# First attention of a two-block transformer kernel: sinks as a score column, one score bank per head, another order in a step, query rounding on GpSimd

## What is computed

```python
def banded_attention(q, k, v, window, rel_table, sinks):
    ...
    def block(args):                     # one block of 128 queries, up to 256 keys
        ...
        s = jnp.einsum('bqhgd,bshd->bhgqs', qn, kn).astype(jnp.float32) + bias
        mask = in_win & (start - n_prev * BLOCK_Q + kj >= 0)
        s = jnp.where(mask, s, NEG_INF)
        ...
            sk = sinks.astype(jnp.float32).reshape(hkv, g_sz, 1, 1)
            m = jnp.maximum(jnp.max(s, axis=-1, keepdims=True), sk)
            e = jnp.exp(s - m)
            p = e / (jnp.sum(e, axis=-1, keepdims=True) + jnp.exp(sk - m))
        return jnp.einsum('bhgqs,bshd->bqhgd', p.astype(vn.dtype), vn)
```

## Time and profile before

| what | us |
|---|---|
| timed runs | 2120.36, 2120.88, 2125.22 |
| their median | 2120.88 |
| the profiled execution: its span, first to last instruction | 2123.0 |
| TensorE busy, whole span | 1988.0 (94%) |
| VectorE, ScalarE, GpSimd busy, whole span | 1021.4, 852.1, 797.5 |
| first attention, first score matmul to the projection's first matmul | 78.9 to 173.4 |
| DMA landing: one piece of raw queries; one bias tile | 2.9; 2.9 |

### The profile page before, as it was taken

How to read it: one execution, slowest core, us unless ns; L and a number is a source line. 1 busy time by engine, 2 the same in 40 slices (tenths; PEclk the granted TensorE clock), 3 DMA queues, 4 the chain that set the end, 5 groups by cost and what they waited for, 6 DMA issues and landing times.

```text
span 2123.0 us, 29194 instructions
## 1 busy us (share of the span) xinstructions
PE 1988.0 (94%) x9640; PEld 1642.4 (77%) x9640; DVE 1021.4 (48%) x2371; ACT 852.1 (40%) x1566; POOL 797.5 (38%) x368
## 2 busy tenths in 40 slices
PE   7889999999999899999999998999999889999896
PEld 5778788888778788878888886877887567777684
DVE  5483765421254767546553216657312664444414
ACT  4463422222343676542222224222223465555523
POOL 3323454444454100126444442545444223242340
PEclk9889999999999899999999999999999989999999
DMA  7432455422333112126553322322322112121121
GB/s 244 127 92 67 150 178 164 138 92 96 99 110 121 36 45 66 42 79 199 176 168 99 99 95 74 106 92 95 99 93 95 43 57 69 40 69 49 60 79 40
DMA packets 70011, 209.40 MB, mean 99 GB/s; under 512 B 9739, under 2 KB 15115, under 8 KB 69948
## 3 DMA queue, kind: packets, MB, share of 16 engines
q1 hardware_dynamic: 57724, 174.72, 25.7%
q10 hardware_dynamic: 12224, 33.85, 5.0%
HBM read 196.90 MB, written 8.49 MB: 97 GB/s over the span
## 4 chain that ended last, share of the span: by engine, by line
PE 58%; issue 21%; DVE 9%; POOL 9%; ACT 2%; DVEq 0%; POOLq 0%; ACTq 0%
PE bank L938 15%; PE bank L939 15%; PE bank L940 15%; POOL wsp L442 9%; PE bank L1215 3%; PE bank L1362 1%; PE bank L1199 1%; PE bank L1381 1%; PE bank L1188 1%; PE bank L1084 1%; PE bank L1373 1%; PE bank L1211 1%; PE bank L972 1%; PE bank L1061 1%; DVE gen L1614 0%
## 5 line engine op out<-in xcount | busy, mean ns | idle before, releaser
L442 POOL TENSOR_TENSOR wsp<-raw,wsp 128x1024 fp32r<-128x1024 f32 x294 | 730.6, 2490 | 1047.9 <-ACT wsp L515 1047.7
L938 PE MATMUL bank<-xs,wsp 128*128 128x512 f32 x1320 | 525.9, 398 | 36.0 <-DVE mid L2040 16.0
L939 PE MATMUL bank<-xs,wsp 128*128 128x512 f32 x1320 | 519.1, 393 | 0.0
L940 PE MATMUL bank<-xs,wsp 128*128 128x512 f32 x1320 | 518.9, 393 | 0.0
L515 ACT ACTIVATE wsp<-raw 128x1024 fp32r<-128x1024 f32 x294 | 307.3, 1052 | 234.4 <-PE bank L940 205.6
L938 PEld LDWEIGHTS bank<-xs,wsp 128*128 128x128 f32 x1320 | 251.3, 190 | 97.0 <-issue 32.3
L938 PE MATMUL bank<-xk,wsp 128*128 128x512 f32 x752 | 295.4, 393 | 9.5 <-DVE xk L1482 5.1
L939 PE MATMUL bank<-xk,wsp 128*128 128x512 f32 x752 | 294.5, 392 | 0.0
L940 PE MATMUL bank<-xk,wsp 128*128 128x512 f32 x752 | 294.4, 391 | 0.0
L940 PEld LDWEIGHTS bank<-xs,wsp 128*128 128x128 f32 x1320 | 250.8, 190 | 53.6
L939 PEld LDWEIGHTS bank<-xs,wsp 128*128 128x128 f32 x1320 | 251.4, 190 | 52.1 <-issue 1.4
(11 more groups left out here) (287 smaller groups left out, 2548.3 us busy)
## 6 DMA issues: line engine op xcount, KB each, us to landing
raw<-weights SPq DMA_DIRECT2D x294, 512.0 KB, 3.3
gen<-ada ACTq DMA_DIRECT2D x48, 512.0 KB, 3.7
tmp<-mid SPq DMA_DIRECT2D x64, 128.0 KB, 2.9
bias_b<-bias_row ACTq DMA_DIRECT2D x1, 4096.0 KB, 37.5
mid<-bias_b SPq DMA_DIRECT2D x8, 512.0 KB, 3.8
hT<-xT SPq DMA_DIRECT2D x2, 1024.0 KB, 10.3
bias_a<-bias_row ACTq DMA_DIRECT2D x1, 2048.0 KB, 16.9
mid<-bias_a SPq DMA_DIRECT2D x8, 256.0 KB, 2.9
```

Of the source, the lines that this page charges most:

```text
L442: pool.tensor_tensor(wsp[:, slot, 1, :], raw[:, slot, :], wsp[:, slot, 0, :].bitcast(F32), ALU.subtract).then_inc(w_ready, 1)
L938: pe.matmul(dst, w[0], x[0], start=first, stop=False)
L939: pe.matmul(dst, w[0], x[1], start=False, stop=False)
L940: return pe.matmul(dst, w[1], x[0], start=False, stop=last)
```

## The change

- The sink becomes column 256 of the score tile. The four score banks hold a zero in that column (four memsets before the stage, counted by `a_zero`), the bias tile holds the sink there (a copy of 128 x 2 per four steps), and the reduction and the Exp run over one column more. L1619, L1621, L1627 and L641 are gone, and `negsink` with them.
- Scores take four banks, one per head and parity (`bank[2 * b + e]`), and each head's scores, reduction and Exp are handed over on their own. Transposes have bank 4 alone, values banks 5 and 6, turned-out blocks bank 7 alone.
- In a slot TensorE does the scores first, then transposes, values and turning out.
- The rounding of queries goes from ScalarE to GpSimd (`pair_queries`), but for the very first pair. GpSimd does copy and subtraction for both heads of a pair in a row, after the scores that last read the old ones.
- SP loads the raw queries first, as soon as GpSimd is done with the old ones, and then the bias tile, each with its own semaphore.
- The two multiplies of `a_outputs` become one over both heads.

```diff
-TQ_A, TQ_B = 5 * 16, 6 * 16
+TQ_A, TQ_B = 4 * 16, 6 * 16
+SINK = 256
...
-        a_s = [gen[:, 1024 + 512 * b:1536 + 512 * b].rearrange("p (e k) -> p e k", e=2) for b in range(2)]
+        a_s = [gen[:, 3328 + 520 * b:3848 + 520 * b].rearrange("p (e k) -> p e k", e=2) for b in range(2)]
...
-                bias, chunk = bias_a[bass.ds((i + 4 * b) * 2, 2)].rearrange("h q y -> q h y"), qT[:, i * 2 + b, :]
+                bias = bias_a[bass.ds((i + 4 * b) * 2, 2)].rearrange("h q y -> q h y")
+                if not isinstance(i, int):
+                    sp.wait_ge(qs_ready, i * 4 + (2 * b - 2))
+                sp.wait_ge(q_ready, b + 1 if isinstance(i, int) else DC)
+                load_queries(b, qT[:, i * 2 + b, :])
                 if not isinstance(i, int):
                     sp.wait_ge(a_s_ready, i * 16 + (8 * b - 8))
-                sp.wait_ge(q_ready, b + 1 if isinstance(i, int) else DC)
-                sp.dma_start(tb[b][:, :, 0:256], bias).then_inc(tq_in[b], 16)
-                load_queries(b, chunk)
+                sp.dma_start(tb[b][:, :, 0:256], bias).then_inc(a_bias_in[b], 16)
...
+            def pair_queries(b, i):
+
+                for e in range(2):
+                    if i or b:
+                        pool.wait_ge(tq_in[b], i * TQ_A + TQ_A)
+                        if i:
+                            pool.wait_ge(a_qk, i * 16 + (8 * b - 8))
+                        pool.tensor_copy(qs[b][e][0], q_raw[b][e]).then_inc(qs_hi, 1)
+                    pool.wait_ge(qs_hi, i * 4 + (2 * b + e + 1))
+                    pool.tensor_tensor(qs[b][e][1], q_raw[b][e], qs[b][e][0].bitcast(F32), ALU.subtract
+                                       ).then_inc(qs_ready, 1)
+
             split_units(0, A_O + AHEAD)
-            queries_lo(0)
+            for n in range(PAIRS):
+                pair_queries(n % 2, n // 2)
...
             def a_soft(m, i):
 
-                b, w = m % 2, (128 if m % 4 == 0 else 256)
-                act.wait_ge(a_nm, i * 8 + (m + 1))
-                for e in range(2):
-                    x = act.activation(a_s[b][:, e, 0:w], a_s[b][:, e, 0:w], ACT.Exp, scale=-1.0,
-                                       bias=stat[:, b, 2 + e:3 + e], accum_out=stat[:, b, 4 + e:5 + e])
-                x.then_inc(a_p, 1)
-                act.wait_ge(a_sk, i * 8 + (m + 1))
-                act.activation(stat[:, b, 8:10], stat[:, b, 6:8], ACT.Exp).then_inc(a_sink, 1)
-
-                if m in (1, 2):
-                    queries_hi(1, m - 1, i * TQ_A + TQ_A)
-                if m in (5, 6) and not (isinstance(i, int) and i > 0):
-                    queries_hi(0, m - 5, i * TQ_A + 2 * TQ_A)
+                b, y0 = m % 2, (P if m % 4 == 0 else 0)
+                for e in range(2):
+                    act.wait_ge(a_s_ready, i * 16 + (2 * m + e + 1))
+                    act.activation(a_s[b][:, e, y0:SINK + 1], a_s[b][:, e, y0:SINK + 1], ACT.Exp, scale=-1.0,
+                                   bias=stat[:, b, e:e + 1], accum_out=stat[:, b, 4 + e:5 + e]).then_inc(a_p, 1)
...
-                act.activation(a_pt[b][:, :, 0:w], bank[2 + b].rearrange("p (e k) -> p e k", e=2)[:, :, 0:w],
+                act.activation(a_pt[b][:, :, 0:w], bank[4].rearrange("p (e k) -> p e k", e=2)[:, :, 0:w],
...
-                k0, w = max(blk - 1, 0) * P, (P if blk == 0 else 2 * P)
+                k0, y0 = max(blk - 1, 0) * P, (P if blk == 0 else 0)
                 for e in range(2):
                     for h in range(2):
-                        x = pe.matmul(bank[b][:, e * 256:e * 256 + w], qs[pp][e][h][:, blk * P:blk * P + P],
-                                      a_ks[:, pp, k0:k0 + w], start=h == 0, stop=h == 1)
-                x.then_inc(a_qk, 1)
+                        x = pe.matmul(bank[2 * b + e][:, y0:SINK], qs[pp][e][h][:, blk * P:blk * P + P],
+                                      a_ks[:, pp, k0:k0 + SINK - y0], start=h == 0, stop=h == 1)
+                    x.then_inc(a_qk, 1)
...
             def a_transpose(m, i):
-                b = m % 2
-                pe.wait_ge(a_p, i * 8 + (m + 1))
-                if again(i, m):
-                    pe.wait_ge(a_pt_ready, i * 8 + (m - 1))
-                for e in range(2):
+                b, y0 = m % 2, (P if m % 4 == 0 else 0)
+                if again(i, m, 1):
+                    pe.wait_ge(a_pt_ready, i * 8 + m)
+                for e in range(2):
+                    pe.wait_ge(a_p, i * 16 + (2 * m + e + 1))
                     for kb in range(1 if m % 4 == 0 else 2):
-                        x = pe.transpose(bank[2 + b][:, e * 256 + kb * P:e * 256 + kb * P + P],
-                                         a_s[b][:, e, kb * P:kb * P + P], ident[:, :])
+                        x = pe.transpose(bank[4][:, e * 256 + kb * P:e * 256 + kb * P + P],
+                                         a_s[b][:, e, y0 + kb * P:y0 + kb * P + P], ident[:, :])
...
-                        x = pe.matmul(bank[4 + b][:, e * HD:e * HD + HD], a_pt[b][:, e, kb * P:kb * P + P],
...
-                    pe.wait_ge(mid_ready, i * 2 + (m // 4 + 1))
-                pe.transpose(bank[6 + m // 4][:, blk * P:blk * P + P], a_o[b], ident[:, :]).then_inc(a_ot, 1)
+                    pe.wait_ge(mid_ready, i * 2 + (m // 4 + 2))
+                pe.transpose(bank[7][:, blk * P:blk * P + P], a_o[b], ident[:, :]).then_inc(a_ot, 1)
...
+            pe.wait_ge(a_zero, 4)
             in_steps(pe, 8, 6, lambda s, i, last: run_slot(
-                ((a_transpose, 2), (a_values, 3), (a_scores, 0), (a_turn_out, 4)), 8, s, i, last))
-            project_out(A_O, DC, XK_A, [0, 1, 2, 3, 4, 5], mid_ready, MID_A + DC)
+                ((a_scores, 0), (a_transpose, 2), (a_values, 3), (a_turn_out, 4)), 8, s, i, last))
+            project_out(A_O, DC, XK_A, [0, 1, 2, 3, 4, 5, 6], mid_ready, MID_A + DC)
...
+            dve.wait_ge(vtok_ready, 1)
+            for n in range(4):
+                dve.memset(bank[n][:, SINK:SINK + 1], 0.0).then_inc(a_zero, 1)
+            dve.wait_ge(a_zero, 4)
+
             def a_bias(m, i):
 
-                b, blk = m % 2, m % 4
-                y0, w = (P, P) if blk == 0 else (0, 2 * P)
-                if blk == 0:
-                    dve.wait_ge(tq_in[m // 4], i * TQ_A + TQ_A)
+                b, pp, y0 = m % 2, m // 4, (P if m % 4 == 0 else 0)
+                if m % 4 == 0:
+                    dve.tensor_copy(tb[pp][:, :, SINK:SINK + 1],
+                                    row("sinks", HEADS)[:, bass.ds(i * 2 + 8 * pp, 2)].unsqueeze(2)).then_inc(a_sink, 1)
+                    dve.wait_ge(a_bias_in[pp], i * 16 + 16)
+                    dve.wait_ge(a_sink, i * 2 + (pp + 1))
                 if again(i, m):
                     dve.wait_ge(a_ptmm, i * 8 + (m - 1))
-                dve.wait_ge(a_qk, i * 8 + (m + 1))
-                dve.memset(stat[:, b, 15:16], 0.0)
-                for e in range(2):
-                    dve.tensor_tensor_reduce(out=a_s[b][:, e, 0:w], in0=bank[b][:, e * 256:e * 256 + w],
-                                             in1=tb[m // 4][:, e, y0:y0 + w], scale=-1.0, scalar=3.0e38, op0=ALU.add,
+                for e in range(2):
+                    dve.wait_ge(a_qk, i * 16 + (2 * m + e + 1))
+                    dve.memset(stat[:, b, 14 + e:15 + e], 0.0)
+                    dve.tensor_tensor_reduce(out=a_s[b][:, e, y0:SINK + 1], in0=bank[2 * b + e][:, y0:SINK + 1],
+                                             in1=tb[pp][:, e, y0:SINK + 1], scale=-1.0, scalar=3.0e38, op0=ALU.add,
                                              op1=ALU.min, accum_out=stat[:, b, e:e + 1]).then_inc(a_s_ready, 1)
-                dve.wait_ge(a_s_ready, i * 16 + 2 * (m + 1))
-                sinks = negsink[:, bass.ds(i * 2 + 8 * (m // 4), 2)]
-                dve.tensor_tensor(stat[:, b, 2:4], stat[:, b, 0:2], sinks, ALU.min).then_inc(a_nm, 1)
-                dve.wait_ge(a_nm, i * 8 + (m + 1))
-                dve.tensor_tensor(stat[:, b, 6:8], stat[:, b, 2:4], sinks, ALU.subtract).then_inc(a_sk, 1)
 
             def a_norm(m, i):
 
                 b = m % 2
-                dve.wait_ge(a_sink, i * 8 + (m + 1))
-                dve.tensor_tensor(stat[:, b, 10:12], stat[:, b, 4:6], stat[:, b, 8:10], ALU.add).then_inc(a_tot, 1)
-                dve.wait_ge(a_tot, i * 8 + (m + 1))
-                dve.reciprocal(stat[:, b, 12:14], stat[:, b, 10:12]).then_inc(a_den, 1)
+                if again(i, m):
+                    dve.wait_ge(a_o_ready, i * 8 + (m - 1))
+                dve.wait_ge(a_p, i * 16 + 2 * (m + 1))
+                dve.reciprocal(stat[:, b, 12:14], stat[:, b, 4:6]).then_inc(a_den, 1)
...
-                for e in range(2):
-                    x = dve.tensor_scalar(a_o[b][:, e * HD:e * HD + HD], bank[4 + b][:, e * HD:e * HD + HD],
-                                          stat[:, b, 12 + e:13 + e], None, ALU.mult)
-                x.then_inc(a_o_ready, 1)
+                by_head = "p (e d) -> p e d"
```

(5 more changed lines are left out.)

12 lines of the change are left out of this document (5 added, 7 removed).

## The result

The changed kernel takes 2102.33 us by median (2101.36 to 2104.09, four runs) against 2123.02 (2120.36 to 2125.22, four runs): a ratio of 0.9901, with a 95% interval from 0.9879 to 0.9922. That is 1.0% faster; the prediction said 2103.3. It had subtracted 17.6 us from 2120.88, the median of three runs of before; with the fourth run that median is 2123.02, and the gain to set beside 17.6 is 20.7 us. The spans of the two profiled executions are 2099.7 and 2123.0 us, 23.3 apart. Two experiments further down each had one execution of several thousand us (5346.80 and 9908.43), which the ratios and the ranges given there leave out. So number and sign were right. The parts were not: the first attention gained twice the forecast, and a stage that the change doesn't touch gave a third of it back.

A forecast was written before the change was run, and what follows sets the result against it. Bound: TensorE at the low clock; at the high clock, ScalarE's wait for VectorE's L1619, held by GpSimd. First-attention groups 80.5 to 62.4 us, 0.5 more at the start: 17.6 off 2120.9 gives 2103.3; range 2096 to 2115.

The forecast's parts named there:

- The sum: First attention, first bias load inside the stage to last reduction: 80.5 us to 62.4, less 0.5 at the start: 17.6 saved.
- Group at the high clock: First attention, four steps at 2.4 GHz: 7.7 us of TensorE work at 94% busy, 8.2 us against 10.2.
- the best end: First attention: 7.7 us a group, no further low stretch, low only till 90 us: 25 us less, 2096.
- Low stretches: First attention at 1.2 GHz, 13.2 us per four steps: low until 93 us, then one further stretch of 7 us.
- (a): First attention: low-clock stretches come as often as before, 29 us; 12 us less, 2109; chance 0.17.
- The start: Ahead of the first attention's loop: four memsets and a semaphore, sink copy 0.3 us; 0.5 us more, first 8.3 us kept.
- What would show it: First attention's signs: bias loads 8 to 8.5 us apart at clock 1.00, TensorE over 93% busy, output projection near 156 us.
- No term of its own: Scores first in the first attention: VectorE's reduction starts some 1.1 us earlier; not priced separately, lets 8.2 be reached.
- (b): First attention: ScalarE becomes the bound at some 2.35 us a step, 9.4 a group; 10.5 us less, 2110; chance 0.05.
- (c): First attention: GpSimd bursts hold VectorE's memset or reciprocal, 10.7 us a group; 5.1 less, 2116; chance 0.07.
- (d): First attention: the clock stays low throughout, 92.4 us; 12 us more, 2133; chance 0.06.
- (e): First attention's saving is lost: output projection waits for weights or GpSimd paces the loop at 10.2; 2119 to 2122; chance 0.06.

The follow-up runs named there:

- with 128 memsets: Changed kernel plus 128 unused one-column VectorE memsets behind the first output projection's inputs, shifting later VectorE code; 2102.91 us (one run).
- in the kernel before with 106: Kernel before the change plus 106 unused VectorE memsets behind the first output projection's inputs; 2134.68 us (one run), against 2123.17 without on the same chip.
- the wait made by hand: Changed kernel with 32 unused VectorE memsets ahead of the second attention, plus four unused 128x480 VectorE additions at each of its three pass beginnings; 2103.84 us.

## Why the prediction was right in its number and not in its parts

**The bound and the mechanism held.** VectorE's two-input minimum, held by GpSimd, stood between scores and exponentials. With the whole change, ScalarE's wait falls from 35.2 to 7.7 us, and the sink column with its banks alone gives 25.3 us. An operation of that kind put back as a dummy costs 6.1. What was shown is thus the lock and the gain of the whole part; the share of the minimum in it was not measured alone.

**The sum was short by 18.3 us in the first attention** (17.6 forecast, 35.9 measured up to the output projection: 173.42 in the earlier trace rows, 137.51 now).

```profile
137.51 0.50 PE L944 MATMUL bank<-xk,wsp 128*128 128x512 f32 x1 [0.27 <-DVE xk L1482]
```

The seven groups from the first bias load of the loop to the last reduction (84.85 to 132.2) took 47.4 us; the forecast was 62.4, and 80.5 stood before. Term by term:

- Group at the high clock: 8.2 us forecast, 47.35 / 7 = 6.76 measured, 7 x 1.44 = 10 us. It was wrong twice. A step's work is 1.87 us and not 2.07: I had added up the weight loads of the earlier trace rows one after the other, values 0.97 and turning out 0.14, and from start to start they are 0.84 and 0.04, since the loads go on beside one another. And the 94% that the second attention reaches is no property of such a loop: there TensorE waits 0.22 + 0.36 + 0.90 us for VectorE in each eight steps (22.6 us), here for nothing (5.00 of 5.00 us). Even the best end, 7.7 a group, was too long.
- Low stretches: 13 us forecast, none measured behind 84 us. They had done 0.98 groups in 13 us, so 13 - 0.98 x 8.2 = 5 us. The link "waits, then a low clock", which rival (a) called loose, holds inside the loop of the second attention nine times of nine for waits of 1.75 to 2.69 us: twice each in the changed kernel, with 128 memsets and in the kernel before with 106, and three times with the wait made by hand. In the first attention it is loose, as (a) had it: with the rounding back on ScalarE three of seven waits of 1.4 to 1.5 us were followed by a fall, and in the kernel before the clock fell at about 100, 113 and 157 us with no single wait of TensorE over 0.7 us near.
- The start: 0.5 us more forecast, 2.4 less measured (first bias load of the loop at 84.85, not 87.20): 3 us. The clock rose at 84, not at 93.

10 + 5 + 3 = 18. The output projection, foreseen near 156 us, started at 137.51.

**The change's price outside its own stage, 12.9 us, was not in the prediction at all.** "What would show it" looked at the first attention only. The sum took what lies behind the stage as moved and otherwise the same; that is the step that failed. 36 us gained and 13 lost make the 23.3 between the spans, near the 17.6 forecast by luck.

**The smaller steps.** GpSimd's copy: 1.27 us guessed (0.61 measured, below the row that I took), hidden either way; a burst is 3.8 us, the low end. One transpose bank for nothing: held, TensorE's transposes waited 0.2 us for ScalarE's turn. The sink copy: 148 to 1230 ns, so its end of 1.3 was real once, at the start; in the loop it took up to 0.47 us, and the loop hides it, as taken. "No term of its own" for scores first: wrong, it is 7.7 us beside GpSimd's rounding and a loss of 5.2 without, and I had tied it to VectorE's early start alone. ScalarE's roundings I gave no term either; on their own they gave 10.4, most of it through the clock.

**The rivals.** (a), as many low stretches as before: none came in this stage. (b), ScalarE as the bound at 9.4 a group: 6.8 were reached, with ScalarE busy 4.5 of 5 us. (c), bursts that hold VectorE: true of the copy alone; what a two-input operation in each step would cost is the 6.1 us of the dummy. (d), the clock stays low: TensorE was busy 5.00 of 5.00 us at 0.50 before 84 us, and the clock rose; it stayed at 1.00 with 4 transposes in each step. By the Trainium skill's rule on transposes (TensorE: Matmul & The Clock Gate, Part 4) I had put 2133 beside it; the trace doesn't bear that out here. (e), a paced loop: copies of 0.61 us, no.

## What to carry to other kernels

A chain between engines in a short step is worth more than its own length when its waits also lower TensorE's clock: read idle times and granted clock together, and price a wait by the two. When an experiment hits the number of a theory, look at its rows too: the rounding alone gave the 2114 us of a theory whose reason the rows don't show. Of two edits in one stage, one can be a loss alone and a gain beside the other (scores first with the sink column: 5.2 us lost before the rounding moved, 7.7 gained after), so try them as a table and not one after the other. And when a change takes code out or puts code in, compare the stages behind it too: look for a loop whose first instruction waits for "issue", and shift it by a few instructions that do nothing.

## What the runs showed of the hardware that I had not expected

- A loop of 284 instructions on VectorE turns in 0.27 to 0.30 us of idle time from the places 2, 34 and 44 (modulo 128 instructions, one kernel each) and in 2.77 to 3.02 us from the place 12 (three kernels). The page shows it as some 10 more packets on the instruction queue.
- A wait of TensorE of 1.75 to 2.69 us inside the loop of the second attention cost 5.6 to 6.8 us each, since the granted clock was at 0.5 for some 10 to 14 us behind it, nine times of nine; idle rows of 0.90 us inside that loop were followed by no fall. In the first attention, waits of 1.4 to 1.5 us were followed by a fall three times of seven.
- A GpSimd copy of 128x512 from fp32 takes 0.61 us, half of a subtraction (1.28).
- A VectorE copy of 128x2 with one SBUF input is stretched beside GpSimd (148 to 1230 ns) as a two-input operation is (150 to 1236 ns), at most to the end of the GpSimd instruction in the cases looked at; memset, reciprocal, and operations with PSUM as one input are not.
